# One of four DRAM block sums of a Winograd matmul is formed in the SBUF staging buffer instead

## The reference

```
x = first_block(x, ...)   # mLSTM + sliding window attention, cross attention to 256 rows, conv FFN
x = second_block(x, ...)  # four mixers of width 256, then relu(h @ w1)^2 @ w2

def conv_ffn(x, w_up, conv_w, conv_b, w_down):
    u = causal_dwconv(x @ w_up, conv_w, conv_b)
    g, val = split(u, 2)
    return (gelu(g) * val) @ w_down          # w_down: 2816 x 1024   ("down")

m = square(relu(h @ mlp_w1[l])) @ mlp_w2[l]  # w1: 1024 x 4096 ("m1"), w2: 4096 x 1024 ("m2")
```

## Time and profile before

| | |
|---|---|
| median of 3 runs | 1231.48 us |
| the profiled execution's own time | 1231.21 us |
| its span | 1229.4 us |
| PE busy | 1222.0 us, 99% |
| DVE busy | 898.7 us, 73% |
| ACT busy | 652.9 us, 53% |
| POOL busy | 56.1 us, 5% |
| transfers of SP's queue | 167.55 MB, 41.0% of 16 DMA engines |
| transfers of POOL's queue | 75.50 MB, 24.7% |

### The profile page before, as it was taken

One profiled execution on the slowest core, in us unless ns is written; L12 is line 12 of the kernel. 1 busy time (PEld: TensorE's weight loads), 2 busy tenths in 40 slices (PEclk: granted clock), 3 DMA queues, 4 the chain that ended last, 5 costly groups with the idle time before them and its releaser, 6 DMA issues.

```text
span 1229.4 us, 17179 instructions
## 1 busy us (share of the span) xinstructions
PE 1222.0 (99%) x6662; PEld 1049.2 (85%) x6662; DVE 898.7 (73%) x1281; ACT 652.9 (53%) x1078; POOL 56.1 (5%) x80
## 2 busy tenths in 40 slices
PE   9999999999999999999999999999999999999998
PEld 9877898898889888888888899778898999988886
DVE  6778887576578656655588587887687777887886
ACT  5565654254546444444566464669354544665654
POOL 0000012000000000000000000000000000000000
PEclk9999999999999999999999999999999999999999
DMA  8445478847635887878575428777737789766572
GB/s 302 144 141 193 162 260 237 275 124 211 179 104 188 212 231 211 200 242 201 212 249 175 140 69 260 204 192 199 245 104 161 261 274 266 254 220 191 172 212 79
DMA packets 63976, 244.53 MB, mean 199 GB/s; under 512 B 6900, under 2 KB 14580, under 8 KB 54424
## 3 DMA queue, kind: packets, MB, share of 16 engines
q1 hardware_dynamic: 53096, 167.55, 41.0%
q0 software_dynamic: 10368, 75.50, 24.7%
q10 hardware_dynamic: 432, 0.39, 0.1%
HBM read 235.55 MB, written 81.26 MB: 258 GB/s over the span
## 4 chain that ended last, share of the span: by engine, by line
PE 99%; DMA 0%; DVE 0%; ACT 0%; issue 0%; DVEq 0%
PE bank L1511 15%; PE bank L1513 15%; PE bank L1512 15%; PE bank L1716 6%; PE bank L1715 6%; PE bank L1717 6%; PE bank L1743 3%; PE bank L1742 3%; PE bank L1741 3%; PE bank L1656 2%; PE bank L1655 2%; PE bank L1660 2%; PE bank L1657 2%; PE bank L1658 2%; PE bank L1659 2%; PE bank L1792 1%
## 5 line engine op out<-in xcount | busy, mean ns | idle before, releaser
L2493 DVE TENSOR_TENSOR wlo<-stage,whi 128x1024 fp32r<-128x1024 f32 (+1 forms) x276 | 332.6, 1211 | 111.7 <-ACT whi L1975 110.4
L1511 PE MATMUL bank<-xh,whi 128*128 128x512 f32 (+1 forms) x944 | 339.1, 359 | 0.2 <-issue 0.2
L1512 PE MATMUL bank<-xl,whi 128*128 128x512 f32 (+1 forms) x944 | 335.2, 355 | 0.0
L1513 PE MATMUL bank<-xh,wlo 128*128 128x512 f32 (+1 forms) x944 | 335.1, 355 | 0.0
L1975 ACT CAST whi<-stage 128x1024 fp32r<-128x1024 f32 (+1 forms) x276 | 284.9, 1039 | 76.6 <-PE bank L1717 27.3
L1511 PEld LDWEIGHTS bank<-xh,whi 128*128 128x128 f32 x944 | 178.3, 189 | 29.7 <-issue 5.3
L1513 PEld LDWEIGHTS bank<-xh,wlo 128*128 128x128 f32 x944 | 178.4, 189 | 25.4
L1512 PEld LDWEIGHTS bank<-xl,whi 128*128 128x128 f32 x944 | 178.4, 189 | 24.6 <-issue 0.2
L1715 PE MATMUL bank<-whi,xh 128*128 128x512 f32 x328 | 127.6, 389 | 0.0
L1716 PE MATMUL bank<-wlo,xh 128*128 128x512 f32 x328 | 127.6, 389 | 0.0
L1717 PE MATMUL bank<-whi,xl 128*128 128x512 f32 x328 | 127.6, 389 | 0.0
(11 more groups left out here) (408 smaller groups left out, 2014.2 us busy)
## 6 DMA issues: line engine op xcount, KB each, us to landing
stage<-in_W_m SPq DMA_DIRECT2D x50, 512.0 KB, 4.1
stage<-in_W_up SPq DMA_DIRECT2D x44, 512.0 KB, 4.4
m_a<-in_W_m POOLq DMA_DIRECT2D x14, 1024.0 KB, 8.2
m_b<-in_W_m POOLq DMA_DIRECT2D x14, 1024.0 KB, 8.2
stage<-in_W_in_a SPq DMA_DIRECT2D x19, 512.0 KB, 4.1
stage<-in_W_down SPq DMA_DIRECT2D x18, 512.0 KB, 4.1
stage<-in_W_out SPq DMA_DIRECT2D x16, 512.0 KB, 5.8
m_c<-in_W_m POOLq DMA_DIRECT2D x7, 1024.0 KB, 5.4
```

Of the source, the lines that this page charges most:

```text
L1511: e.matmul(b[:, cols], hi[:, k, :], xh[:, k, cols], start=(k == 0), stop=False)
L1512: e.matmul(b[:, cols], hi[:, k, :], xl[:, k, cols], start=False, stop=False)
L1513: last = e.matmul(b[:, cols], lo[:, k, :], xh[:, k, cols], start=False, stop=(k == 7))
L2493: e.tensor_tensor(wlo[:, plan.place[i], c], stage[:, i % NSTAGE, c], whi[:, plan.place[i], c].bitcast(F32), ALU.subtract).then_inc(S["w_lo"])
```

## The change

The sum b is no longer made in DRAM. For an r3 chunk SP loads the plain quarter s12 into the stage slot, and then POOL issues an accumulating transfer that adds the quarter s22 from DRAM onto the slot. ACT and DVE wait for both (`arrived`). This removes 2 of the 8 DRAM transfers for each pair of groups, 18 in all (54 are left), and adds 18 accumulating transfers of 512 KB: 4 in down, 6 in m1, 8 in m2. `at(n)` is rewritten for 54: the last DRAM sum is now allowed in out2, so none runs beside m1 or m2. On POOL the staged additions are put among the DRAM sums, as `waiting` says; those of m1 and m2 come after all of these. Each waits for its own load and for the staged addition before it.

```diff
-COPIES = (("a", "s11"), ("b", "s12"), ("c", "s22"), ("d", "s21"))
-ADDS = (("a", "s12"), ("b", "s22"), ("c", "a"), ("d", "c"))
+COPIES = (("a", "s11"), ("c", "s22"), ("d", "s21"))
+ADDS = (("a", "s12"), ("c", "a"), ("d", "c"))
+STAGED = {"b": ("s12", "s22")}
...
+        def second_part(i):
+            block = chunk_of(*CHUNKS[i])
+            if block and TIMES[block[0]] in STAGED:
+                return quarter(CHUNKS[i][0], STAGED[TIMES[block[0]]][1])[block[1]]
+        def staged(i):
+            return S["staged"], 16 * sum(second_part(k) is not None for k in range(i + 1))
+        def arrived(q, i):
+            q.wait_ge(s_stage[i % NSTAGE], 16 * (i // NSTAGE + 1))
+            if second_part(i) is not None:
+                q.wait_ge(*staged(i))
...  ACT's and DVE's split(i)
-                q.wait_ge(s_stage[s], 16 * (i // NSTAGE + 1))
+                arrived(q, i)
...  SP's chunk(i)
                         kind, g = TIMES[block[0]], block[1]
+                        kind = STAGED.get(kind, (kind,))[0]
...  POOL
             def at(n):
-                if n < 9:
+                if n < 4:
                     return CHUNK0["kv_k"]
-                if n < 17:
-                    return CHUNK0["xq"] + n - 8
-                if n < 43:
-                    return CHUNK0["up"] + 2 + 8 * (n - 17) // 5
-                if n < 61:
-                    return CHUNK0["in2_c"] + 1 + (n - 43)
-                if n < 64:
-                    return CHUNK0["m1"] + 3 + 2 * (n - 61)
-                return CHUNK0["m1"] + PLAIN + 2 + 4 * (n - 64)
+                if n < 12:
+                    return CHUNK0["xq"] + n - 3
+                if n < 38:
+                    return CHUNK0["up"] + 2 + 8 * (n - 12) // 5
+                return CHUNK0["in2_c"] + 1 + 3 * (n - 38) // 2
+            def add_staged(i):
+                q.wait_ge(s_stage[i % NSTAGE], 16 * (i // NSTAGE + 1))
+                sem, n = staged(i)
+                if n > 16:
+                    q.wait_ge(sem, n - 16)
+                e.dma_start(stage[:, i % NSTAGE, :], second_part(i), accum_op=ALU.add).then_inc(sem, 16)
+            waiting = [i for i in range(len(CHUNKS)) if second_part(i) is not None]
             def add_up(lo, hi):
                 for n, (block, part, (name, w), more) in enumerate(ORDER):
                     if lo <= n < hi:
+                        while waiting and waiting[0] - NSTAGE - NSPLIT < at(n):
+                            add_staged(waiting.pop(0))
...
-                add_up(2 * h, 2 * h + 2)
-            add_up(8, len(ORDER))
+                add_up(h, h + 1)
+            add_up(4, len(ORDER))
+            while waiting:
+                add_staged(waiting.pop(0))
```

More of the change, by code:

```diff
@@ L1231 @@
 SEMAPHORES = (
-    ["st0", "st1", "st2", "st3"] + [f"ld_x{k}" for k in range(5)]
+    ["st0", "st1", "st2", "st3", "staged"] + [f"ld_x{k}" for k in range(5)]
     + ["ld_w0", "ld_xf", "w0_lo", "ld_xr", "ld_c", "ld_masks", "ld_bias", "ld_mem", "ld_rows",
@@ L1477, in chunk_of @@
             return SEVEN[name][c] if name in SEVEN and c < len(SEVEN[name]) else None
-        def sum_ready(name, kind, g):
[L1480 to L1484, removed]
+        def second_part(i):
[8 more added lines that the diff above has]
+                q.wait_ge(*staged(i))
+        def sum_ready(name, kind, g):
+            return 16 * [(o[0], o[1], o[2][0], o[3]) for o in ORDER].index((name, g // 2, kind, 1)) + 16
         sums = {(m, n): nc.dram_tensor(f"{m}_{n}", (k, 128, 1024), F32, kind="Internal").ap()
-                for m, k in GROUPS.items() for n in "abcd"}
+                for m, k in GROUPS.items() for n in "acd"}
         def quarter(name, n):
@@ L2489, in split @@
             def split(i):
-                q.wait_ge(s_stage[i % NSTAGE], 16 * (i // NSTAGE + 1))
+                arrived(q, i)
                 q.wait_ge(S["w_hi"], i + 2)
```

## The result

The changed kernel takes 1285.96 us (median, 1284.45 to 1290.16) against 1231.48 before: ratio 1.045, 95% interval 1.0432 to 1.0467, 54 to 55 us slower. The forecast was 1244 with a range of 1232 to 1262: the sign is right, the size is not, and the time lies outside the range.

What follows compares the result with a forecast made beforehand. The prediction took PE, busy 1222.0 of 1229.4 us, as the only bound. Losses of 10.4 us in m2 and 2.5 in down, 12.9 together, on 1231.2 gave 1244 us, range 1232 to 1262.

Steps and rivals of the forecast that it cites:

- P: Period from one b chunk's load to the next through the stage slot, forecast 12.2 us against 10.9 of PE's work.
- PE bounds the kernel and the removed traffic is worth 0: Whole kernel: PE alone sets the time, so taking out 18 DRAM transfers of 1 MB gives 0.
- Rival 3: Kernel gets faster: DRAM sums slow PE's pace slightly, and fewer give it back, to 1228.5 us; chance 4%.
- A loop through one stage slot: In m2 and down each b chunk's load waits for the previous b chunk's split; 1.3 us too slow each.
- The addition at 5.2: A 512 KB addition into SBUF takes 5.2 us: 4.9 from halving a DRAM addition, 0.3 for meeting one load.
- v behind five splits: Before part two of m2 and down, DVE reaches v's end 11.2 us after the last b chunk's low part.
- j1's activations: Start of m2: activations stand behind j3's split on ACT and DVE, so PE stops for 2 us at j1.
- the 10.4: PE's forecast lateness in us at j32 of m2, where v is done at 1168.7; contains earlier losses in m2.
- m1 at 0: In m1 b is every seventh chunk, so nothing adds up: cost 0, with idle time covering additions up to 6 us.
- down at 2.5: In down the same loop with four b chunks makes PE 2.5 us late at j16.
- j7: b chunk of down whose addition waits behind DRAM sums; forecast landed by about 616, cast at 620.80, cost 0.
- Rival 1: The addition is as short as a plain load, 4.2 us or less, giving 1234.1 or 1232 us; chance 17%.

Runs made afterwards that it cites:

- thin: The changed kernel with the a, c and d chunks of down, m1 and m2 loaded with 128 of their 1024 columns: 1247.31 us, ratio 1.0136.
- alternate: The changed kernel with the staged additions of every second b chunk left out, 9 of 18: 1249.81 us, ratio 1.0142.
- plain: The changed kernel with the staged additions made transfers of the same 512 KB that add nothing and overwrite: 1260.11 us, ratio 1.0234.
- half: The changed kernel with staged additions of only the first 512 columns, 256 KB each: 1259.91 us, ratio 1.0226.
- hold: The changed kernel, complete, with SP holding the load two chunks after a b chunk until that chunk's addition has landed: 1265.11 us, ratio 1.0277.
- v moved: The changed kernel, complete, with four of the five splits that DVE does ahead of v put behind it: 1286.34 us, ratio 1.0453.
- the first experiment: The changed kernel without the 18 staged additions and the waits for them, b chunks loaded as the plain quarter s12: 1231.21 us, ratio 0.9998.
- only m2 kept: The changed kernel with the staged additions of down and m1 left out, 8 of 18 remaining: 1264.24 us, ratio 1.0267.
- only m1 kept: The changed kernel with the staged additions of down and m2 left out, 6 of 18 remaining: 1241.46 us, ratio 1.0084.

## Why the forecast was right in kind and wrong in size

| kernel | P in m2, us | slower by, us |
|---|---|---|
| forecast | 12.2 | 12.9 |
| thin | 12.02 | 16.0 |
| alternate | 12.0 | 18.5 |
| plain | 12.94 | 28.6 |
| half | 13.0 | 28.4 |
| hold | 13.04 | 33.8 |
| the change | 14.57 | 54.5 |
| v moved | 14.5 | 55.0 |

- **PE bounds the kernel and the removed traffic is worth 0.** Right, shown by the first experiment (0.9998). Rival 3 falls with it.
- **A loop through one stage slot.** Right, shown by the period on POOL's timeline and by the loss rising with P, though P alone does not fix it (28.6 and 33.8 at 12.9 and 13.0). The release of a slot and what follows it also came out as taken: 2.43 against 2.4.
- **The addition at 5.2.** This is the step that failed, by its last term. "4.9, and 0.3 for meeting one other load": the 4.9 measures 5.4 alone, and the 0.3 measures 2.2 for one load and 3.8 for two. I read that other loads keep the engines 65.9% busy and did not turn it into a price, though the earlier trace rows had DRAM additions from 7.7 to 11.9 us, a spread that asked for a reason. Load and waking were together 3.9 in place of 4.5, which gave 0.6 of it back. P came out at 14.57 in m2, 2.4 us more, which over eight periods is 19 us. In down the two periods took 15.6 each (j11's load took 6.0, its addition 6.9, j15's addition 9.2), 7 us more. Together that is 26 of the 42 us missed.
- **v behind five splits.** Right: 11.7 against 11.2. m2 checks with the measured P: j3's load is issued at 1081.49, eight periods of 14.6 and 11.7 more are 1210.0, and PE starts j32 at 1210.34. Thin checks the whole chain at the forecast's P: in its profiled execution (1250.1 us) PE is 3.5 us late at j16 of down and 9.4 at j32 of m2, where 2.5 and 10.4 were forecast; the clock behind these two stops is 4.1 more, the rest lies elsewhere.
- **j1's activations.** Right in place. The forecast was 2 us inside the 10.4; it is 8.2. From j3's load at 1081.49 to its cast at 1094.78 it is 13.3 where 9.8 was taken (load 4.3, addition 8.6), and from there to the activation 6.5 where 6.2 was. The rest is a premise that failed: j3's load was to be "set by splits that the change doesn't move". It was issued 11.3 us ahead of PE's j0 before and is issued 8.9 ahead of it now, behind m1's last addition. 2.0 + 3.5 + 0.3 + 2.4 is the 8.2. Where m1 has no additions (only m2 kept) the load is again 11.3 ahead and the stop 5.3 in place of 8.0.
- **m1 at 0.** Wrong. I had written that an addition over 6 us eats a lead, and "nothing below about 9". In the change those of 8.1 and 8.2 cost nothing and those of 8.9 and 9.0 stopped PE for 1.0 and 2.1 us; but one of 7.6 there cost 0.3, and in other runs one of 8.0 (only m1 kept) cost 0.9 and one of 7.8 (v moved) 0.6. So the bound was about 1 us too high; the forecast's own terms give 8.4 + 1.3 + 2.9 from load to need, less 4.6 for the rest, about 8. That additions would reach it was excluded only by the mis-sized term.
- **down at 2.5.** 10.0 at j16 and 2.2 of lower clock behind it: the 2.5, the 7 us of the two longer periods and 0.4 at v are the 10.0. j7 was not missed: its addition landed at 615.2, and it was cast at 619.8.
- **A stop costs its length.** A term left out. After a long stop PE runs at 1.2 GHz for a while, and its busy time grew by 14.6 us by it. Not all of that is loss of its own. In m2 j32 starts when v is done, and the check above reaches 1210.0 with no term for PE's pace; so the 7 us of lower clock within part one are contained in v's lateness, as the shorter stops there are. What adds to the time is the clock behind the two v stops (2.2 and 2.7) and in m1 (2.6, within its 7.0).
- **The sum again.** Of the 42 us missed, 26 are the longer periods, 7.0 m1, 4.9 the clock behind the v stops, 2.4 the late start of j3's load and about 1 the way from the last b chunk to v: 41. The terms are read from the trace; that they may be added like this is an estimate.
- **Rival 1's argument.** "Sooner than copies in DRAM even per byte" misreads: the shortest load, 3.1 us for at most 512 KB, is 6.2 us or more a MB, the shortest copy 5.2. It changed no term of the sum.

What stays open: how the 8.0 us of m2 divides among the three loads that an addition meets was not measured apart, nor whether they meet in the DMA engines or in the memory behind them. Of the versions tried that compute the reference, none beats the kernel before, and with PE at 1222.0 of 1229.4 us there none that only rearranges transfers had much to win.

## What to carry to other kernels

Where a change makes a second transfer follow a first through the same buffer, price the whole loop through that buffer (load, wake, second transfer, use, next load) against the pace of the engine that it feeds, and multiply the excess by the number of turns. Take the transfer's length in the company it will have, from rows in which as many others run: a length measured alone or scaled by bytes is a lower bound, and when the sum moves by ten us for each us of one term, that term is to be bounded from a crowded row. Check also the start of the loop: what the same change does just ahead of it can move it. And where the bounding engine would start to stop, add the matmuls at the lower clock behind a long stop, unless something else already makes the engine late at the next place.

## What the runs showed of the hardware

- An accumulating transfer suffers more from company than a plain one, most of all from the first load: one load of SP beside it makes 512 KB go from 5.4 to 7.6 us, a plain one from 3.9 to 4.8; two make them 9.2 and 6.9, three 10.2 and 7.9. SP's own load goes from 3.8 alone to 5.2 beside the addition. The Trainium skill, DMA: Bandwidth & Descriptors, "Queues, rings and completion order", has each DMA engine take turns between the queues that have work; the runs agree in that both sides slow down, but they don't tell this way of sharing from another, and the page has no price for it.
- An addition into DRAM takes about as long as one into the SBUF: 7.6 against 7.9 us for 1 MB, 6.0 against 5.4 for 512 KB. A DRAM copy of 1 MB takes 4.9 alone; the least seen in the kernel before was 5.2.
- After a stop of 6.69 us PE started twelve matmuls 0.42 to 0.43 us apart before it was back at 0.23, with a granted clock of 0.50 from 1210.3 to 1215.5.
